# Attention scores from queries and keys split into upper and lower parts

## The reference

```python
q, k, v = jnp.split(h @ w_qkv, 3, axis=-1)      # 8 heads, 2 parts each, 64 wide
q = partial_rope(q, cos, sin); k = partial_rope(k, cos, sin)
s = einsum('bhcqd,bhckd->bhcqk', qb, kb) * scale     # per block of 128 queries
p = softmax(where(mask, s, NEG_INF))
a = p[:, :, 0] - lam * p[:, :, 1]
o = einsum('bhqk,bhkv->bhqv', a, vb)            # then a norm per head and h @ w_o
```

## Time and profile before

| | |
|---|---|
| median of 3 runs | 1490.82 us (1487.9 to 1491.02) |
| the profiled execution | 1489.55 us, span 1487.7 us |
| mean granted TensorE clock | 0.953 of full |
| busy: PE, PEld, DVE, ACT, POOL | 93%, 88%, 63%, 55%, 7% |
| chain that ended last | PE 73%, DVE 13%, ACT 9%, issue 4%, DMA 1% |
| two costliest lines of the chain | L1660 18%, L1662 18% |

### The profile page before, as it was taken

One profiled execution on the slowest core, in us unless ns is written; L12 is line 12 of the kernel. 1 busy time (PEld: TensorE's weight loads), 2 busy tenths in 40 slices (PEclk: granted clock), 3 DMA queues, 4 the chain that ended last, 5 costly groups with the idle time before them and its releaser, 6 DMA issues.

```text
span 1487.7 us, 27408 instructions
## 1 busy us (share of the span) xinstructions
PE 1387.8 (93%) x10038; PEld 1312.4 (88%) x10038; DVE 938.9 (63%) x1550; ACT 812.8 (55%) x1573; POOL 97.7 (7%) x101
## 2 busy tenths in 40 slices
PE   6999999989999999999999997999998976789997
PEld 6999999989999999999987877999996865668877
DVE  5777448857776367774465545777635563555774
ACT  6767535357766467665444446766644430256663
POOL 2000001011000010000010002100000040010000
PEclk9999999999999999999989998999998975799999
DMA  5766645645666527676333313666642630135431
GB/s 194 250 211 248 213 149 150 189 130 196 239 215 242 177 83 249 213 248 212 119 114 100 100 43 117 210 225 224 246 156 81 186 111 0 51 101 161 128 113 44
DMA packets 63166, 239.39 MB, mean 161 GB/s; under 512 B 7009, under 2 KB 8433, under 8 KB 62961
## 3 DMA queue, kind: packets, MB, share of 16 engines
q1 hardware_dynamic: 63024, 238.31, 48.3%
q0 software_dynamic: 64, 0.02, 0.0%
HBM read 237.24 MB, written 1.05 MB: 160 GB/s over the span
## 4 chain that ended last, share of the span: by engine, by line
PE 73%; DVE 13%; ACT 9%; issue 4%; DMA 1%; DVEq 0%; ACTq 0%; SPq 0%
PE bank L1660 18%; PE bank L1662 18%; PE bank L1661 17%; PE bank L1667 6%; DVE w_lo L990 4%; ACT w_hi L567 3%; PE bank L1668 3%; ACT ada_raw L647 2%; PE bank L2016 2%; PE bank L1733 1%; PE bank L1734 1%; PE bank L1726 1%; DMA ada_raw<-ada_w 1%; ACT arena L934 1%; DVE ada_raw L1078 1%
## 5 line engine op out<-in xcount | busy, mean ns | idle before, releaser
L990 DVE TENSOR_TENSOR w_lo<-raw,w_hi 128x1024 fp32r<-128x1024 f32 (+1 forms) x376 | 494.7, 1319 | 337.9 <-ACT w_hi L567 337.7
L1660 PE MATMUL bank<-x_hl,w_hi 128*128 128x272 f32 (+1 forms) x1672 | 488.1, 292 | 14.8 <-DVE w_lo L990 14.5
L567 ACT ACTIVATE w_hi<-raw 128x1024 fp32r<-128x1024 f32 (+1 forms) x376 | 414.2, 1106 | 144.2 <-PE bank L1662 131.2
L1662 PE MATMUL bank<-x_hl,w_lo 128*128 128x272 f32 (+1 forms) x1672 | 483.2, 289 | 0.0
L1661 PE MATMUL bank<-x_hl,w_hi 128*128 128x272 f32 (+1 forms) x1672 | 481.7, 288 | 0.0
L1660 PEld LDWEIGHTS bank<-x_hl,w_hi 128*128 128x128 f32 x1672 | 317.7, 190 | 17.5 <-ACT arena L603 8.6
L1661 PEld LDWEIGHTS bank<-x_hl,w_hi 128*128 128x128 f32 x1672 | 320.1, 191 | 0.6
L1662 PEld LDWEIGHTS bank<-x_hl,w_lo 128*128 128x128 f32 x1672 | 317.2, 190 | 0.0
L1660 PE MATMUL bank<-a_hi,w_hi 128*128 128x272 f32 (+1 forms) x960 | 280.5, 292 | 14.7 <-DVE a_lo L1102 2.9
L1662 PE MATMUL bank<-a_hi,w_lo 128*128 128x272 f32 (+1 forms) x960 | 277.3, 289 | 0.0
L1661 PE MATMUL bank<-a_lo,w_hi 128*128 128x272 f32 (+1 forms) x960 | 276.9, 288 | 0.0
(11 more groups left out here) (286 smaller groups left out, 1395.9 us busy)
## 6 DMA issues: line engine op xcount, KB each, us to landing
raw<-w SPq DMA_DIRECT2D x312, 512.0 KB, 4.3
raw<-w SPq DMA_DIRECT2D x64, 704.0 KB, 4.7
ada_raw<-ada_w SPq DMA_DIRECT2D x48, 512.0 KB, 3.6
h<-x_in SPq DMA_DIRECT2D x1, 1088.0 KB, 5.2
cst<-consts SPq DMA_DIRECT2D x1, 560.0 KB, 4.6
out<-h SPq DMA_DIRECT2D x1, 512.0 KB, 2.9
out<-h SPq DMA_DIRECT2D x4, 128.0 KB, 2.1
poolw<-pool_w SPq DMA_DIRECT2D x1, 256.0 KB, 4.9
```

What stands on the lines that cost most here:

```text
L567: sc.activation(w_hi[:, s, 0:n], raw[:, s, 0:n], ACT.Copy).then_inc(w_hi_ready, 1)
L990: ve.tensor_tensor(w_lo[:, s, 0:n], raw[:, s, 0:n], w_hi[:, s, 0:n].bitcast(F32), ALU.subtract).then_inc(w_lo_ready, 1)
L1660: te.matmul(dst, w_hi[:, s, a:a + P], rhs_hi, start=first, stop=False)
L1662: return te.matmul(dst, w_lo[:, s, a:a + P], rhs_hi, start=False, stop=last)
```

## The change

Behind the rotation, ScalarE now writes the upper parts of the rotated queries and keys of a head (`qk_upper`: two copies, to two unused chunks of the `a_hi` buffer), and VectorE their lower parts (`qk_lower`: two subtractions, to `a_lo`). `scores` waits for the last subtraction instead of the rotation and replaces each full-format product by three split passes; the mask products stay where they are. In the written order, `qk_upper(p-1)` stands on ScalarE behind the weight split of unit 3p+1 and ahead of the copies `attn_t(p-2)`; `qk_lower(p-1)` stands on VectorE behind `value(p)` and ahead of the weight split of unit 3p+2.

```diff
+        q_hi, q_lo, k_hi, k_lo = a_hi[:, DC, 0:SEQ], a_lo[:, DC, 0:SEQ], a_hi[:, DC + 1, :], a_lo[:, DC + 1, :]
...
+            def qk_upper(h):
+                sc.wait_ge(vec.sem, vec.at(f"rope{h}", "ks"))
+                sc.activation(q_hi, q_rot[h % 2][:, 0:SEQ], ACT.Copy).then_inc(act.step(f"qkh{h}", "q"), 1)
+                sc.activation(k_hi, k_rot[h % 2], ACT.Copy).then_inc(act.step(f"qkh{h}", "k"), 1)
...
                     att_split(u + 1)
+                if head(p - 1):
+                    qk_upper(p - 1)
                 if head(p - 2):
                     attn_t(p - 2)
...
+            def qk_lower(h):
+                ve.wait_ge(act.sem, act.at(f"qkh{h}", "k"))
+                ve.tensor_tensor(q_lo, q_rot[h % 2][:, 0:SEQ], q_hi.bitcast(F32), ALU.subtract).then_inc(vec.step(f"qkl{h}", "q"), 1)
+                ve.tensor_tensor(k_lo, k_rot[h % 2], k_hi.bitcast(F32), ALU.subtract).then_inc(vec.step(f"qkl{h}", "k"), 1)
...
                     value(p)
+                if head(p - 1):
+                    qk_lower(p - 1)
+                if head(p):
                     att_split(u + 2)
...
+            def score_part(dst, rows, q, k):
+                te.matmul(dst, q_hi[rows, q], k_hi[rows, k], start=True, stop=False)
+                te.matmul(dst, q_hi[rows, q], k_lo[rows, k], start=False, stop=False)
+                te.matmul(dst, q_lo[rows, q], k_hi[rows, k], start=False, stop=False)
+
             def scores(h):
                 b = h % 2
-                te.wait_ge(vec.sem, vec.at(f"rope{h}", "ks"))
+                te.wait_ge(vec.sem, vec.at(f"qkl{h}", "k"))
                 for c in range(2):
...
-                    te.matmul(dst[:, 0:KA], q_rot[b][rows, 0:P], k_rot[b][rows, 0:KA], start=True, stop=False)
+                    score_part(dst[:, 0:KA], rows, slice(0, P), slice(0, KA))
                     te.matmul(dst[:, META:KA], ident_b[:, :], causal_b[:, :], start=False, stop=True)
-                    te.matmul(dst[:, KA:KA + T], q_rot[b][rows, P:SEQ], k_rot[b][rows, 0:T], start=True, stop=False)
+                    score_part(dst[:, KA:KA + T], rows, slice(P, SEQ), slice(0, T))
```

More of the change, by code:

```diff
@@ L344, in build @@
             if head(p - 1):
+                vec.phase(f"qkl{p - 1}", ["q", "k"])
+            if head(p - 1):
                 vec.phase(f"max{p - 1}", ["mA0", "mB0", "mA1", "mB1", "n"])
@@ L356, in build @@
                 act.phase(f"k{p}", ["k"])
+            if head(p - 1):
+                act.phase(f"qkh{p - 1}", ["q", "k"])
             if head(p - 2):
```

## The result

| | before | changed |
|---|---|---|
| median | 1489.38 us (7 runs) | 1493.61 us (7 runs) |
| ratio to before | | 1.002, 95% interval 1.001 to 1.0029 |
| profiled execution, span | 1489.55 us, 1487.7 us | 1491.74 us, 1489.9 us |
| first channel swap to last head sum | 136.1 us (755.35 to 891.42) | 140.0 us (757.11 to 897.12) |

The change makes the kernel slower: the medians are 4.2 us apart, and the ratio of the runs says 0.1 to 0.3%. The spans of the two traces differ by 2.2 us only, but the stage that was changed by 3.9 us: in the changed trace the part ahead of the first swap is 1.8 us longer and the part behind the last head sum 3.5 us shorter, though the change touches neither. Low-clock stretches lie at other places there in the two traces.

What follows compares the result with a forecast made beforehand. TensorE, busy for 93% of the span, was taken as the bound; +2.4 - 0.6 + 0.1 = +1.9 us on the profiled 1489.55 gives 1491.5, and the median's 1.3 us more makes 1492.7 us, range 1489.3 to 1500.5.

Steps and rivals of the forecast that it cites:

- Score products in the steady periods: TensorE, seven heads at full clock: 144-column block 0.48 us, 272-column block 0.58; -0.09 us a head, -0.6 us in all.
- (a): Rival, TensorE's 144-column blocks: narrow split passes go at the full format's rate; 1500.4 us, chance 0.25.
- (b): Rival, TensorE's score blocks: weight loads don't hide, each pass 0.11 us of load plus its stream; 1497.3 us, chance 0.12.
- (c): Rival, score blocks: bare load and gap belong to the full format, not the rows, and go; 1486.3 us, chance 0.06.
- Copies and subtractions: New ScalarE copies and VectorE subtractions in steady periods: cost nothing, some 0.2 us of cover each; 0.9 us kept for upper end.
- First head: Scores of head 0 on TensorE: no cover, start 2.2 us later, more of them at low clock; +2.4 us.
- two cases: Low clock behind the first head's idle time: back at 772.6 as now, +1.6 us, or a 10.2 us stretch, +3.2 us.
- Last head: ScalarE's copies of head 6's weights wait for the keys' rotation and end at 879.4, wanted at 879.28; +0.1 us.
- limit of 0.2%: Whole kernel: a time within 0.2% (3 us) of before cannot be told from it.
- the forecast's own range: Whole kernel, forecast's mechanism with the first head dearer or cheaper: 1489.5 to 1495.5 us, elsewhere from 1489.3; chance 0.57.

Runs made afterwards that it cites:

- halved weights: Changed kernel, but passes two and three of each narrow block take 64 of the 128 queries; one execution, 1494.68 us.
- full products behind all the new work: Changed kernel with copies, subtractions and later wait kept, but score products in full format from the unsplit queries and keys; ratio 1.002 to the kernel before.
- changed twice: Two traces of the changed kernel: the first series, and a repeat with no edit, ratio 1.003 to the kernel before.
- four passes more: Kernel before with heads 1 to 7 split, head 0 full, and four passes of projection unit 9 done twice; one profile, stage 136.2 us.
- masks behind each part: Kernel before, full format, with both score blocks of a part one behind the other, then its two masks; ratio 0.9964, median 1483.37 us.
- all masks last: Kernel before, full format, with all four score blocks of a head first, then all four masks; 1474.36 us, ratio 0.9899.

## Why the prediction held, point by point

- **Score products in the steady periods.** Forecast 0.48 and 0.58 us for the blocks, 0.09 us less a head; measured 0.49 and 0.58, 0.07 to 0.08 less, and so 0.6 for the seven. That narrow passes wait for their loads is shown by the halved weights. Of the rivals, (a) falls with 0.06 to 0.07 us for 144 columns and (b) with 0.11 us from pass to pass. (c) falls because split blocks keep the gap (0.15 us behind each mask in both), and because it leaves when the masks do, in either format. The rule of the Trainium skill ("TensorE: Matmul & The Clock Gate", "What overlaps and what doesn't") that a load hides only under another row group doesn't hold here: 0.11 us from pass to pass leaves no room for load and stream in a row.
- **Copies and subtractions.** Forecast nothing, with 0.2 us of cover each; shown by the full products behind all the new work (16.72 us a period).
- **First head.** The mechanism was right: idle 3.55 us against a forecast of 3.6, scores 2.2 us late. The term was mis-sized: 2.4 us was the middle of two cases, and it was the dearer one: swap 0 to swap 1 is 3.1 to 3.3 us longer in four traces with this stall, masks between and the blocks whole (changed twice, only head 0 split, full products behind the new work), and the low stretch is 10.2 us long in all four.
- **Last head.** Forecast +0.1; with full products behind all the new work, the only change from swap 7 to the last head sum is +0.2 us (20.77 against 20.59). For the changed kernel 0.1 comes off again for head 7's own scores.
- **Not forecast.** The low-clock stretch at 873 us, which costs the stage about 1.1 us (0.6 + 0.5 in the table, against -0.1 and +0.1 with the four passes more, where it is absent). The prediction took the steady heads to keep the full clock, since the trace of before showed them so; this term it put at nothing.

The sum by these parts is 3.2 - 0.6 + 0.2 + 1.1 = 3.9 us, as the stage has it; forecast were 1.9. The time itself, 1493.61 us against a forecast of 1492.7, came nearer than the change did, and that is luck: the forecast was built on a median of 1490.82 us of three runs, where the seven give 1489.38, and this 1.4 us made up for part of the rise that was missing. By the prediction's own limit of 0.2% the result lies at the edge: the ratio is 1.002, with an interval from 0.1 to 0.29%. In its working, the forecast's own range ends at 1489.5 us in one place and at 1489.3 in another. What stays open is why the clock falls near 873 us, and whether the format has a part in it beyond the moment at which the head comes.

## What to carry to other kernels

A format with fewer cycles per column gained nothing where weight loads set the pace: 0.11 us a load against 0.06 us of stream. Before a change of format in a pipelined stage, look for the one iteration without the neighbour that hides the new step: here it cost more than five times what the other seven gave (3.2 against 0.6 us). One trace with a low-clock stretch and one without it do not show what brought it: look at several executions, and at where the clock's changes fall in each. And where products use half the rows, put those of both halves next to each other, with nothing of full height between.

## What the runs showed of the hardware that was not expected

Two score parts on rows 0 to 63 and 64 to 127, issued one behind the other with no mask between, run at the same time: 0.91 us for both instead of 0.90 us each (799.73 to 800.63 in the full kernel with masks behind each part). The Trainium skill has this ("TensorE: Matmul & The Clock Gate", "Part 3: Packing small matmuls — row/col tiling"): tiles in distinct row groups run concurrently; these traces agree. What they add is the price of a 128-row product between: it costs 0.15 us for itself and its switch, and takes the pairing away. Without the masks between the parts a period fell from 16.12 to 15.12 us.

The clock's low stretches went with small shifts in time: a head that came 83.2 to 83.5 us after the clock was back at its full level met a low stretch of 3.4 to 6.8 us, at 83.7 to 84.4 us none did, in the nine traces of the table, though nothing in the program marks either moment. And the same idle time before the first scores (1.38 us) was followed by 6.8 us at the low level in the kernel before, by 3.4 us with the masks behind each part, and by none with all masks last.
